# Short conv taps shared out over GpSimd, ScalarE and VectorE, and out-projection tiles read from PSUM by halves, in a hybrid decoder layer

## What is computed

```
h = modulate(rmsnorm(x, g_pre_mix), sh1, sc1)
z = h @ w_in                                    # gb, gc, v | a, g
y_short = gb * (causal_dwconv(gc * v, w_short, b_short))     # width 3
u = layernorm(causal_dwconv(a * sigmoid(g), w_cfm_dw))       # width 31
y = per_head_rmsnorm(concat([y_short, silu(u)]))
x = x + gt1 * rmsnorm(y @ w_out, g_post_mix)    # out-projection
h = modulate(rmsnorm(x, g_pre_ffn), sh2, sc2)
x = x + gt2 * rmsnorm((silu(h @ w_gate) * (h @ w_up)) @ w_down, g_post_ffn)
```

## Time and profile before

| | |
|---|---|
| median of 3 runs | 773.74 us (773.06 to 774.92) |
| profiled execution: its own time | 773.06 us |
| span of its slowest core (core 2) | 771.5 us (all cores: 765.1 to 771.5) |
| PE / DVE / ACT / POOL busy in the span | 95% / 41% / 35% / 18% |
| share of the chain that ended last: PE | 87% |

### The profile page before, as it was taken

One profiled execution on the slowest core, in us unless ns is written; L12 is line 12 of the kernel. 1 busy time (PEld: TensorE's weight loads), 2 busy tenths in 40 slices (PEclk: granted clock), 3 DMA queues, 4 the chain that ended last, 5 costly groups with the idle time before them and its releaser, 6 DMA issues.

```text
span 771.5 us, 11238 instructions; the slowest of 8 cores (765.1 to 771.5 us)
## 1 busy us (share of the span) xinstructions
PE 732.8 (95%) x4139; PEld 367.2 (48%) x4139; DVE 314.6 (41%) x489; ACT 268.7 (35%) x460; POOL 135.5 (18%) x271
## 2 busy tenths in 40 slices
PE   0979999999998799999999999999999999999996
PEld 0667468554443335544444444444444444444442
DVE  2333665876898765554122131222212122112222
ACT  1444548895477654434111110111111111111112
POOL 4533203322114152433010010000000000000000
PEclk9989899999999899999999999999999999999999
DMA  8999637897595568889985385333434432001322
GB/s 177 196 241 204 114 77 120 130 182 138 116 229 161 158 143 212 187 195 207 194 166 117 56 140 133 110 110 109 110 55 82 83 61 50 0 1 56 109 82 83
DMA packets 36807, 98.17 MB, mean 127 GB/s; under 512 B 4112, under 2 KB 12432, under 8 KB 33424
## 3 DMA queue, kind: packets, MB, share of 16 engines
q0 software_dynamic: 20048, 66.92, 45.8%
q1 hardware_dynamic: 16704, 30.52, 12.4%
HBM read 125.54 MB, written 16.78 MB: 184 GB/s over the span
## 4 chain that ended last, share of the span: by engine, by line
PE 87%; DMA 5%; ACT 2%; issue 2%; DVE 1%; POOL 1%; DVEq 0%; ACTq 0%; POOLq 0%
PE ps L579 86%; DMA wag_73<-wag 5%; PE ps L758 1%; POOL small L599 1%; ACT rs_119 L591 1%; ACT hT L591 0%; ACT xn_98 L591 0%; DVE pga_127 L595 0%; ACT xn_99 L591 0%; ACT xn_97 L591 0%; DVE xc_84 L595 0%; DVE xc_86 L595 0%; DVE xc_85 L595 0%; DVEq L419 0%; DVE yT L595 0%
## 5 line engine op out<-in xcount | busy, mean ns | idle before, releaser
L579 PE MATMUL ps<-hT,slot_46 128*128 128x512 bf16 x512 | 114.1, 379 | 0.2 <-issue 0.2
L579 PE MATMUL ps<-wdn_65,actT 128*128 128x512 bf16 x512 | 113.3, 379 | 0.0
L579 PE MATMUL ps<-hT,slot_43 128*128 128x512 bf16 x448 | 100.5, 379 | 0.0
L579 PE MATMUL ps<-hT,slot_45 128*128 128x512 bf16 x448 | 100.3, 379 | 0.0
L579 PE MATMUL ps<-hT,slot_44 128*128 128x512 bf16 x384 | 84.3, 379 | 0.4 <-ACT xn_99 L591 0.4
L579 PEld LDWEIGHTS ps<-wdn_65,actT 128*128 128x128 bf16 x512 | 50.1, 98 | 60.4
L579 PEld LDWEIGHTS ps<-hT,slot_46 128*128 128x128 bf16 x512 | 49.9, 98 | 58.9 <-issue 1.1
L579 PEld LDWEIGHTS ps<-hT,slot_43 128*128 128x128 bf16 x448 | 43.6, 98 | 52.2 <-issue 0.3
L579 PEld LDWEIGHTS ps<-hT,slot_45 128*128 128x128 bf16 x448 | 43.5, 98 | 50.0
L599 POOL TENSOR_SCALAR small<-small 128x1 f32<-128x1 f32 x62 | 16.3, 263 | 283.8 <-ACT xn_96 L591 138.1
L579 PEld LDWEIGHTS ps<-hT,slot_44 128*128 128x128 bf16 x384 | 37.4, 98 | 46.0 <-issue 0.8
(11 more groups left out here) (330 smaller groups left out, 961.9 us busy)
## 6 DMA issues: line engine op xcount, KB each, us to landing
slot_46<-wgu POOLq DMA_DIRECT2D x6, 1024.0 KB, 10.4
slot_44<-wgu POOLq DMA_DIRECT2D x6, 1024.0 KB, 10.1
slot_45<-wgu POOLq DMA_DIRECT2D x5, 1024.0 KB, 14.5
slot_43<-wgu POOLq DMA_DIRECT2D x5, 1024.0 KB, 8.6
wdn_65<-wdn POOLq DMA_DIRECT2D x16, 256.0 KB, 14.3
slot_44<-wada POOLq DMA_DIRECT2D x12, 256.0 KB, 9.4
slot_43<-wada POOLq DMA_DIRECT2D x2, 1024.0 KB, 12.2
slot_45<-wada POOLq DMA_DIRECT2D x8, 256.0 KB, 15.9
```

The costliest lines, as they stand in the source:

```text
L579: return P.op("pe", lambda e: e.matmul(out.ap, lhsT=lhsT.ap, rhs=rhs.ap, start=start, stop=stop), reads=[lhsT, rhs] + list(reads), writes= ...
```

## The change

Tap 2 becomes a plain product on POOL into a buffer of its own, `acp` (one, laid over staging buffers of an earlier stage); tap 0 stays on ACT; POOL adds acp to acc; DVE adds tap 1 last. In `post` of the out-projection (`l == 0`) the product and the square are each done by halves of 512 columns, one bank each: DVE begins with the half 0 while ACT squares half 1, then they change over. The two sums of squares are added inside POOL's first one-column operation. `PAD` is 20 in place of 40, and with all costs the scheduler's order is made anew.

```diff
+        acp_s = sb_space("acp", 1, 512, F32, at=cur[0] - 4096)
         acc_s = sb_space("acc", 2, 512, F32)
...
-            ac = Tile(acc_s).v()
-            for d in range(3):
+            ac, a2 = Tile(acc_s).v(), Tile(acp_s).v()
+            for d in (2, 0, 1):
...
+                to = a2 if d == 2 else ac
...
-                    if d == 0:
+                    if d == 2:
+                        P.op("pool", lambda e, dst=dst, src=src, w=w: e.tensor_scalar(out=dst.ap, in0=src.ap, scalar1=w, scalar2=0.0, op0=ALU.mult, op1=ALU.add),
+                             reads=[src, K_V], writes=[dst], cost=60 + 1.05 * n * PT, lat=80.0, name="sconv")
+                    elif d == 0:
...
+                if d == 0:
+                    P.op("pool", lambda e: e.tensor_tensor(out=ac.ap, in0=ac.ap, in1=a2.ap, op=ALU.add),
+                         reads=[ac, a2], writes=[ac], cost=60 + 1.4 * 512, lat=80.0, name="sadd")
...
+            if l == 0:
+                tt = Tile(pg_s[l])
+                tv = tt.v()
+                for z in range(2):
+                    for y, hv_ in ((z, "g"), (1 - z, "s")):
+                        a, b = 512 * y, 512 * y + 512
+                        ph = pv(a, b, part=y)
+                        if hv_ == "g":
+                            th, gh = tt.v(a, b, part=y), gtg[l].v(a, b)
+                            dve("tensor_tensor", [ph, gh], [th], 690, "po_g", out=th, in0=ph, in1=gh, op=ALU.mult)
+                        else:
+                            c = SM_SSQ + i if y else SM_SS2
+                            act(View(lambda a=a, b=b: junk.ap[:, a:b], junk.keys, junk.tile), ph, AF.Square, scale=1.0 / 32.0, accum=sm(c),
+                                writes=[("ssq", i) if y else ("ssh", 0)], name="po_sq")
+                pool("tensor_scalar", [("ssq", i), ("ssh", 0)], [("ss2", i)], 350, "po_rs", out=sm(SM_SSQ + i), in0=sm(SM_SSQ + i), scalar1=EPS,
+                     scalar2=sm(SM_SS2), op0=ALU.add, op1=ALU.add)
...
-                post(pt.v(), xt, 0, 16 + i, xb_.v())
+                post(pt.v, xt, 0, 16 + i, xb_.v())
...
-PAD = 40
+PAD = 20
```

More of the change, by code:

```diff
@@ L548, in build_program @@
         shb = buf("shb", 8, BF16)
-        small = buf("small", 208, F32)
-        SM_EPS, SM_EXP, SM_SH, SM_GS, SM_T, SM_SSQ, SM_RS, SM_BI = 0, 1, 2, 18, 34, 50, 114, 178
+        small = buf("small", 209, F32)
+        SM_EPS, SM_EXP, SM_SH, SM_GS, SM_T, SM_SSQ, SM_RS, SM_BI, SM_SS2 = 0, 1, 2, 18, 34, 50, 114, 178, 208
         psum = [es.enter_context(nc.psum_tensor("ps%d" % i, [128, 1024], F32)) for i in range(4)]
@@ L1051, in taps @@
                     src = View(rows2(cvb[j], o) if n == 2 else cvb[j].t[:, o:o + PT], ks)
-                    dst = View(lambda x=x, n=n: ac.ap[:, x * PT:(x + n) * PT] if n == 1 else pair_of(ac), ac.keys, ac.tile)
-                    if d == 0:
+                    dst = View(lambda x=x, n=n, to=to: to.ap[:, x * PT:(x + n) * PT] if n == 1 else pair_of(to), to.keys, to.tile)
+                    if d == 2:
+                        P.op("pool", lambda e, dst=dst, src=src, w=w: e.tensor_scalar(out=dst.ap, in0=src.ap, scalar1=w, scalar2=0.0, op0=ALU.mult, op1=ALU.add),
+                             reads=[src, K_V], writes=[dst], cost=60 + 1.05 * n * PT, lat=80.0, name="sconv")
+                    elif d == 0:
                         act(dst, src, AF.Identity, reads=[K_V], scale=w, bias=vc(V_BSH + j), npt=2, name="sconv")
@@ L1087, in post @@
         def post(pv, xt, l, i, junk):
+            if l == 0:
[14 more added lines that the diff above has]
+                     scalar2=sm(SM_SS2), op0=ALU.add, op1=ALU.add)
+                pool("tensor_tensor", [("ss2", i), ("mhalf",)], [("rs", i)], 640, "po_rs", out=sm(SM_RS + i), in0=sm(SM_SSQ + i), in1=sm(SM_EXP),
+                     op=ALU.pow)
+                dve("scalar_tensor_tensor", [tv, ("rs", i), xt], [xt], 1290, "po_add", out=xt, in0=tv, scalar=sm(SM_RS + i), in1=xt,
+                    op0=ALU.mult, op1=ALU.add)
+                return
             tv = Tile(pg_s[l]).v()
```

## The result

The changed kernel takes 785.94 us (median), the kernel before 773.57 on the same chip: a ratio of 1.0156, 95% interval 1.0136 to 1.0176. It is slower by 12 us, where 769.0 was forecast and 774.5 was the upper end. One of its four executions (804.23) fell in a slower state, which executions of the kernel before show too, and the ratio leaves it out. The profiled execution shown here took 786.14, its span is 784.6.

A forecast was written before the change was run, and what follows sets the result against it. The prediction took PE waiting for DVE at the short convolution's end as the bound. Gains of 1.9 + 0.9 + 2.0 = 4.8 us from a 773.74 median gave 768.9, stated as 769.0, range 764.5 to 774.5.

The forecast's parts named there:

- What bounds the kernel: End of the short convolution: PE waits for busy DVE before quarter 0's last xn; 10.05 us could be won in all.
- Taps, the price on GpSimd: Tap 2 on POOL: product 0.58, sum 0.94, so 1.52 us a tap; upper bounds 1.16 and 1.88.
- Collisions: DVE instructions with two SBUF inputs meeting POOL's reads, first product to last xn: 1.4 us, bounds 0 and 7.6.
- the bounds of 219.5 and 223.5: Start of DVE's first out-projection product, put at 221.5 behind two yT that wait for ACT, with these as limits.
- The ten instructions: DVE's list from first product to last xn loses ten instructions of 0.66 us each, 6.6 us.
- Halves: Out-projection: a tile's product and square take 1.4 us side by side instead of 2.2, for 0.3 more over four tiles.
- The 4.8 us: Whole forecast gain: 1.9 at quarter 0's transposes and seven matmuls, 0.9 from the clock, 2.0 from later waits.
- PAD at nothing: Other moves from the new PAD cost nothing; in the width-31 convolution 0.5 us is left between square and matmul.
- Rival (3): POOL becomes the bound: loss from 3.0 us a tap; at 3.5 it costs 3.5, 777.3 us; chance 0.13.
- The sign that I named for being wrong: POOL taps of 3 us or more, DVE taps or adds beyond 1 us, or PE waiting in projections before the out-projection.

The follow-up runs named there:

- 1.82 us a tap: Changed kernel with GpSimd's product replaced by one memset and its sum by two, tap 2 left out of the output: 771.27 us, ratio 0.9969.
- 2.46 a tap: Changed kernel with GpSimd's product replaced by two memsets and its sum by two, tap 2 left out of the output: 775.97 us, ratio 1.0036.
- 3.1 us a tap: Changed kernel with GpSimd's product replaced by two memsets and its sum by three, tap 2 left out of the output: 785.90 us, ratio 1.0147.

## Why the prediction was wrong

- **What bounds the kernel**: right. The time is decided where PE waits for VectorE's list in the out-projection of quarter 0; with the list shorter and GpSimd out of the way (1.82 us a tap, no reads) the kernel gains 0.3%, half of what was forecast.
- **Taps, the price on GpSimd**: failed. 1.52 us was taken, from two rows of 128 columns and of one. Alone it is 0.70 + 1.27, with the 0.17 between them 2.14, and beside VectorE 2.6. The upper bounds, 1.16 and 1.88, held the averages; the value between them was taken too low, and the gap between two dependent instructions of one engine was left out. The estimate from the Trainium skill, GPSIMD Engine Reference, Elementwise side-by-side cycle accounting, 1.11 for the sum, was nearer than my 0.94, and still below 1.27. From 1.82 to 2.46 a tap, 5.2 us.
- **Collisions**: failed, and the larger part as far as the runs separate it from the length. 1.4 us was taken, of bounds 0 to 7.6, for 13 chance meetings of half a tap each. Between the first product and the last xn it was 3.9, and that counted only part of the place: ahead of the first product another 3.9 us of stretched instructions and 4.3 of waits for sums (204.85 to 225.60) put that product at 229.04, outside the bounds of 219.5 and 223.5. Those bounds were made from PE and two yT, as if the taps ahead of it cost VectorE nothing; PE, held up there too, had the tile ready at 224.4 and not at 219.5, and VectorE took it 4.6 later still. A meeting costs more than half a tap, too: the add stood for 0.98, a yT for 1.0.
- **The ten instructions**: VectorE does lose them, 16 in all, but its busy time in the whole kernel went from 314.6 to 316.6 us: what was taken off came back as stretch and as halves. From the first product to the last xn it took 31.8 us, as before (32.06), and not 27.2.
- **Halves**: the 0.8 a tile was right, 0.72 measured, and that the two engines read PSUM side by side without harm too (0.69 and 0.60 side by side). The 4.8 us along with the taps were not met even without reads (2.4), since the halves' own waits from 300 on, put at nothing, took some 2. By themselves the halves gave nothing until their planned price was mended.
- **PAD at nothing**: wrong in both directions, a gain of 0.24% in the kernel before and a loss of 0.6% with the halves. (Under this head sets a square of sq_121 beside a matmul of sq_120; its own matmul starts at 122.43, so 0.8 and not 0.5 was left. Nothing came of it.)
- **Rival (3)** had the direction, with a wrong mechanism and price: it put the loss from 3.0 us a tap, 3.5 us of it at 3.5. The real taps stayed under that, at 2.6, and lost 12. Without any reads it was 2.8 us at 2.46 and 11.4 at 3.1. It asked when GpSimd would be through with its last sum. But VectorE stands still at each sum that is late, and what stands behind it loses, long before GpSimd is full. The sign that I named for being wrong, PE waiting in the projections ahead of the out-projection, is there: 2.29 at 217.56. So is a tap beyond 1 us, 1.76; for the adds that sign could not serve, as they take 1.28 in the earlier trace rows already.

Open: how the 9.3 us divide between stretch, the last 0.13 of length and the order around the first product; what the whole change would take with the halves' mended prices; and why one PAD suits an order and the other doesn't. No run takes these apart.

## What to carry to other kernels

Work moved to GpSimd is not work removed from VectorE, if it reads SBUF while VectorE runs instructions with two SBUF inputs: price it by its own length and by what it does to VectorE's, and look first for rows of VectorE beside wide GpSimd work; if there are none, a kernel with added, unused work there gives a bound on the price in one run. A step that goes through a third engine is paid at every wait of an engine that takes its list in order, not only when the third engine is full. And where a scheduler makes the order, tell it the measured prices before judging an edit: that alone turned the halves from 0.25% slower to 0.4% faster.

## What the runs showed of the hardware

- GpSimd, 128 x 512: product of bf16 into f32 0.70 us alone, sum of two f32 tiles 1.27, memset 0.53 (two in a row 1.17); some 0.17 us between two dependent ones (0.12 between memsets).
- VectorE and GpSimd hold each other up when both read SBUF and VectorE has two inputs there: 0.75 became up to 1.93 (a yT at 211.64), 1.28 up to 2.26, GpSimd's 1.27 up to 2.17. With a memset on GpSimd a tap stayed at 745 ns. ysh, with one input in PSUM, took 0.75 at most between 195 and 270.
- xn, a tensor_scalar from f32 to bf16 with one SBUF input, is held up as well: 1.43 (row 259.40), and by memsets too a little, 0.92 against 0.75 in the kernel with 3.1 us a tap.
